# High and low halves of the input in one 512-column product, in two mixer projections and the MLP's first layer

## What is computed

```python
u = rmsnorm(h, mix_norm_w[l])
p = u @ w_in[l]
o_dn = deltanet_group(p[..., :DN_COLS], ...)     # causal conv of 4 taps and silu on q, k, v
o_rw = rwkv7_group(p[..., DN_COLS:], ...)        # p + (token_shift(p) - p) * mu
h = h + concatenate([o_dn, o_rw], -1) @ w_out[l]
h = h + memory_cross_attention(...)
h = h + square(relu(rmsnorm(h, ffn_norm_w[l]) @ ffn_w1[l])) @ ffn_w2[l]
```

## Time and profile before

| what | value |
|---|---|
| runs of the kernel before | 2596.57 us median of 3 (2587.17 to 2599.15) |
| span of the profiled execution | 2589.5 us (the page gives no other time for this execution) |
| TensorE busy | 2270.6 us, 88% |
| VectorE busy | 1329.3 us, 51% |
| ScalarE busy | 796.3 us, 31% |
| mean granted clock of TensorE | 0.919 of 2.4 GHz |
| DeltaNet projection, first to last product | 34.5 to 226.2 us |
| RWKV projection, first to last split product | 313.3 to 454.1 us |
| MLP, first product of the first layer | 972.1 us |

### The profile page before, as it was taken

The page is one execution under the profiler, slowest core; times in us unless marked ns, Lnnn a source line. Parts: engine busy times, 40 slices in busy tenths (PEclk is TensorE's granted clock), DMA queues, the critical chain, the costliest instruction groups (busy, mean ns, idle before and its releaser), DMA issues. The chain is left out here.

```text
span 2589.5 us, 39793 instructions
## 1 busy us (share of the span) xinstructions
PE 2270.6 (88%) x17044; PEld 1833.3 (71%) x17044; DVE 1329.3 (51%) x1574; ACT 796.3 (31%) x933; POOL 21.5 (1%) x62
## 2 busy tenths in 40 slices
PE   7998799788799969999999999969884768888885
PEld 7998799577777649998999989958743424344441
DVE  4776655554452136979788888855532211111112
ACT  4453333311233034334343343454502101111110
POOL 0000000000000000000000000000000000000000
PEclk8999899887799989999999999999997788999997
DMA  5443034100143317988888988843405499999998
GB/s 203 177 195 131 2 138 187 57 2 1 40 189 130 130 76 294 352 320 323 307 327 312 344 320 341 308 164 137 195 1 212 183 429 428 427 422 427 427 427 338
DMA packets 68150, 610.05 MB, mean 236 GB/s; under 512 B 9614, under 2 KB 9870, under 8 KB 16782
## 3 DMA queue, kind: packets, MB, share of 16 engines
q1 hardware_dynamic: 56906, 572.11, 55.3%
q0 software_dynamic: 1872, 23.07, 2.2%
q10 hardware_dynamic: 9216, 12.60, 1.4%
HBM read 674.85 MB, written 14.68 MB: 266 GB/s over the span
## 5 line engine op out<-in xcount | busy, mean ns | idle before, releaser
L2051 ACT ACTIVATE ffn_w_hi<-ffn_raw 128x2048 fp32r<-128x2048 f32 x128 | 245.0, 1915 | 372.1 <-PE psum L2096 368.8
L2058 DVE TENSOR_TENSOR ffn_w_lo<-ffn_raw,ffn_w_hi 128x2048 fp32r<-128x2048 f32 x128 | 292.9, 2292 | 90.7 <-ACT ffn_w_hi L2051 90.7
L2094 PE MATMUL psum<-u_hi,ffn_w_hi 128*128 128x256 f32 x1024 | 293.9, 287 | 15.0 <-DVE ffn_w_lo L2058 13.9
L2805 PE MATMUL psum<-moe_raw,moe_x_t 128*32 128x512 f32 x1536 | 217.3, 697 | 91.2 <-DMA moe_raw<-in_moe 83.7
L2096 PE MATMUL psum<-u_hi,ffn_w_lo 128*128 128x256 f32 x1024 | 293.3, 286 | 0.0
L2095 PE MATMUL psum<-u_lo,ffn_w_hi 128*128 128x256 f32 x1024 | 293.3, 286 | 0.0
L613 DVE SCALAR_TENSOR_TENSOR shared<-mod_raw,c_silu,shared 128x2048 f32<-128x2048 f32 x96 | 225.6, 2350 | 0.0
L2094 PEld LDWEIGHTS psum<-u_hi,ffn_w_hi 128*128 128x128 f32 x1024 | 200.4, 196 | 15.8 <-DVE ffn_w_lo L2058 14.1
L2095 PEld LDWEIGHTS psum<-u_lo,ffn_w_hi 128*128 128x128 f32 x1024 | 200.2, 196 | 0.4
L2096 PEld LDWEIGHTS psum<-u_hi,ffn_w_lo 128*128 128x128 f32 x1024 | 200.2, 196 | 0.0
L2094 PE MATMUL psum<-ffn_w_hi,ffn_hid_hi 128*128 128x512 f32 x512 | 199.4, 390 | 0.0
(11 more groups left out here) (563 smaller groups left out, 4348.2 us busy)
## 6 DMA issues: line engine op xcount, KB each, us to landing
moe_raw<-in_moe SPq DMA_DIRECT2D x96, 2048.0 KB, 17.7
ffn_raw<-in_ffn SPq DMA_DIRECT2D x128, 1024.0 KB, 5.2
ring<-in_stream SPq DMA_DIRECT2D x59, 2048.0 KB, 12.3
mod_raw<-in_mod SPq DMA_DIRECT2D x96, 1024.0 KB, 7.4
moe_raw<-in_moe POOLq DMA_DIRECT2D x48, 2048.0 KB
expert_rows<-moe_stage ACTq DMA_DIRECT2D x192, 64.0 KB, 8.7
x<-in_x SPq DMA_DIRECT2D x2, 1024.0 KB, 5.8
u<-in_mem SPq DMA_DIRECT2D x2, 1024.0 KB, 15.7
```

Of the source, the lines that this page charges most:

```text
L2051: act.activation(self.w_hi[:, number % self.HIGHS], self.raw[:, number % self.RAWS], ACT.Copy)\
L2058: dve.tensor_tensor(self.w_lo[:, number % self.LOWS], self.raw[:, number % self.RAWS], self.w_hi[:, number % self.HIGHS].bitcast(F32), ALU ...
L2094: pe.matmul(out, lhs[0], rhs[0], start=start, stop=False)
L2805: mm = pe.matmul(summed(tile)[strip(q), :], e.x_t[:, tile // 4 % 2, UNIT_KC * u + c, strip(tile % 4)], w[:, c * COLS:(c + 1) * COLS], star ...
```

## The change

In three places the input's high and low parts now lie side by side, chunk by chunk, in one tile of [128, 16, 2, 256]. For the high weights one product of 512 columns over both parts writes a whole bank: columns 0 to 255 hold high x high, columns 256 to 511 high x low. The low weights' product of 256 columns adds to columns 0 to 255. So there are two products per chunk in place of three, and two half banks to be added: ScalarE copies the right half out of PSUM (`rest`), VectorE adds the left half to it (`total`).

```diff
 class SplitTiles:
+        self.u = sb(f"{name}_u", [P, KC, 2, T], F32R)
+        self.u_hi, self.u_lo = self.u[:, :, 0, :], self.u[:, :, 1, :]
+        self.rests = sb(f"{name}_rests", [P, 2, T], F32)
...
-                pe.matmul(out, hi, self.u_hi[:, chunk, :], start=chunk == 0, stop=False)
-                pe.matmul(out, hi, self.u_lo[:, chunk, :], start=False, stop=False)
-                mm = pe.matmul(out, lo, self.u_hi[:, chunk, :], start=False, stop=chunk == KC - 1)
+                pair = self.u[:, chunk].rearrange("p a t -> p (a t)")
+                if chunk == KC - 1:
+                    pe.matmul(both[:, 0:T], lo, self.u_hi[:, chunk, :], start=False, stop=False)
+                    mm = pe.matmul(both, hi, pair, start=False, stop=True)
+                else:
+                    pe.matmul(both, hi, pair, start=chunk == 0, stop=False)
+                    mm = pe.matmul(both[:, 0:T], lo, self.u_hi[:, chunk, :], start=False, stop=False)
...
+    def rest(self, act, x, turn=None):
+        k, at = self.k, self.at
+        act.wait_ge(k.ft_free, at(turn, 8, self.f0 + 3 + x))
+        act.wait_ge(k.ft_done, at(turn, 8, self.f0 + x + 1))
+        act.activation(self.rests[:, x % 2], bank(k, x % 4)[:, T:2 * T], ACT.Copy).then_inc(k.piece_rest, 1)
+
+    def total(self, dve, x, out=None, turn=None):
+        k = self.k
+        dve.wait_ge(k.piece_rest, self.at(turn, 8, self.p0 + x + 1))
+        rest = self.rests[:, x % 2]
+        return dve.tensor_tensor(rest if out is None else out, bank(k, x % 4)[:, 0:T], rest, ALU.add)
...
 deltanet_project, VectorE
             tiles.low(dve, 0, (0, 1))
+            tiles.low(dve, 1, (0,))
             with dve.Fori(0, 3) as i:
-                s.loop(i, 8 * 4)
+                s.loop(i, 8 * 5)
                 for m in range(8):
-                    tiles.low(dve, m + 1, (0,), turn=i)
-                    dve.wait_ge(k.ft_done, i * 8 + f0 + m + 1)
-                    ps = bank(k, m % 4)
+                    tiles.low(dve, m + 1, (1,), turn=i)
+                    s.step(tiles.total(dve, m, turn=i))
+                    s.settle()
+                    ps = tiles.rests[:, m % 2]
...
-                        if lag == 2:
-                            tiles.low(dve, m + 1, (1,), turn=i)
+                        if lag == 3:
+                            tiles.low(dve, m + 2, (0,), turn=i)
...
 deltanet_project, ScalarE
                     tiles.high(act, m + 1, (1,), turn=i)
+                    tiles.rest(act, m, turn=i)
                     tiles.high(act, m + 2, (0,), turn=i)
-                    act.wait_ge(k.dve_sem, i * 32 + d0 + 4 * (m + 1))
+                    act.wait_ge(k.dve_sem, i * 40 + d0 + 5 * (m + 1))
...
 mlp, ScalarE
-                act.activation(f.hid[:], k.psum[:, 0:4, 0:T], ACT.Relu).then_inc(f.taken, 1)
+                act.activation(f.hid[:], k.psum[:, 0:4, T:2 * T], ACT.Copy).then_inc(k.act_sem, 1)
+
+            def squares(e):
                 act.wait_ge(f.taken, e + 1)
+                act.activation(f.hid[:], f.hid[:], ACT.Relu).then_inc(k.act_sem, 1)
+                act.wait_ge(k.act_sem, rectified(e))
                 act.activation(f.hid[:], f.hid[:], ACT.Square).then_inc(f.squared, 1)
...
 mlp, VectorE
+            def total(e):
+                dve.wait_ge(k.act_sem, rest(e))
+                dve.tensor_tensor(f.hid[:], k.psum[:, 0:4, 0:T], f.hid[:], ALU.add).then_inc(f.taken, 1)
```

More of the change, by code:

```diff
@@ L314, in product @@
         pe.wait_ge(k.ft_free, at(turn, 8, self.f0 + x + 1))
-        out = bank(k, x % 4)[:, 0:T]
+        both = bank(k, x % 4)
         for half in range(2):
@@ L862, in _ @@
                     tiles.low(dve, m + 1, (1,))
-                dn.dve_after(dve, m)
+                dn.dve_after(dve, m, tiles)
             s.settle()
@@ L882, in _ @@
                     tiles.high(act, m + 1, (1,))
+                tiles.rest(act, m)
                 dn.act_between(act, m)
@@ L1168, in _ @@
             tiles.input_high(act, u)
-            with act.Fori(0, 3) as i:
+            tiles.high(act, 0, (0, 1))
+            tiles.high(act, 1, (0,))
+            with act.Fori(0, 2) as i:
                 for m in range(8):
-                    tiles.high(act, m, (0, 1), turn=i)
+                    tiles.high(act, m + 1, (1,), turn=i)
+                    tiles.rest(act, m, turn=i)
+                    tiles.high(act, m + 2, (0,), turn=i)
+            for m in range(16, 24):
+                if m < 23:
+                    tiles.high(act, m + 1, (1,))
+                tiles.rest(act, m)
+                if m < 22:
+                    tiles.high(act, m + 2, (0,))
         @block.vector
@@ L1186, in _ @@
             tiles.low(dve, 0, (0, 1))
+            tiles.low(dve, 1, (0,))
             with dve.Fori(0, 2) as i:
-                s.loop(i, 8)
+                s.loop(i, 16)
                 for m in range(8):
-                    tiles.low(dve, m + 1, (0,), turn=i)
-                    dve.wait_ge(k.ft_done, i * 8 + f0 + m + 1)
-                    shift(bank(k, m % 4), k.one_less_mu[:, bass.ds(i * 8 + m, 1)],
+                    tiles.low(dve, m + 1, (1,), turn=i)
+                    s.step(tiles.total(dve, m, turn=i))
+                    s.settle()
+                    shift(tiles.rests[:, m % 2], k.one_less_mu[:, bass.ds(i * 8 + m, 1)],
                           k.cols[:, bass.ds(i * 8 + (COL["mu"][0] + m), 1)],
@@ L1199, in _ @@
                 if m < 23:
[L1200 to L1203, removed]
                     tiles.low(dve, m + 1, (1,))
+                s.step(tiles.total(dve, m))
+                s.settle()
+                shift(tiles.rests[:, m % 2], k.one_less_mu[:, m:m + 1], col(k, "mu", m), mix[:, m, :], mix[:, m, 1:T])
+                if m < 22:
+                    tiles.low(dve, m + 2, (0,))
             for m in range(2):
@@ L2153, in _ @@
                 f.split_high(act, number)
+                if number >= 6:
+                    e, j = order[number - 2]
+                    if (e, j) == (1, 0) or (j == f.HALVES and e < FFN_BLOCKS - 1):
+                        squares(0 if j == 0 else e + 1)
                 mod.copy_after(act, number)
@@ L2171, in _ @@
                     e, j = order[number - 2]
-                    if (e, j) == (1, 0) or (j == f.HALVES and e < FFN_BLOCKS - 1):
-                        hidden(0 if j == 0 else e + 1)
+                    due = 0 if (e, j) == (1, 0) else e + 1 if j == f.HALVES and e < FFN_BLOCKS - 1 else None
+                    if due is not None:
+                        total(due)
                     e, j = order[number - 3]
@@ L2177, in _ @@
                 f.split_low(dve, number)
+                if number >= 6 and due is not None:
+                    hidden(due)
                 mod.sum_after(dve, number)
```

40 lines of the change are left out of this document (25 added, 15 removed).

## The result

The changed kernel takes 2604.53 us (median of 9 runs, 2601.48 to 2616.89), the kernel before 2593.98 (9 runs, 2587.17 to 2600.66) on the same chip: ratio 1.0049 (95% interval 1.003 to 1.0067), which is some 13 us more by the ratio, 10.6 between the medians, inside the range and within 0.5%. The profiled execution of the changed kernel took 2601.8 us, span 2600.1. That the forecast of 2600.7 came so near is partly luck: the median of three runs that it started from was 2.6 us above that of nine, and of the change it had +4.1.

A forecast was written before the change was run, and what follows sets the result against it. The prediction took TensorE to bound the three stages before the change. DeltaNet's loop +23.3, its last tiles -1.7, RWKV -5.1 and MLP -12.4 made +4.1 us on 2596.6, so 2600.7 us, range 2580 to 2618.

The forecast's parts named there:

- the ring: DeltaNet loop: ScalarE and VectorE wait on each other from SiLU to SiLU, 6.53 us per tile against 5.76 before.
- Table loads: DeltaNet loop: ScalarE's table reloads, 1.28 us each, are now paid in the ring, 5 x 1.28 = 6.4 us.
- The first two tiles still run on weights split ahead: DeltaNet loop: only 22 of 24 tiles pay the ring's longer step, 16.9 us.
- the z tiles: Last 8 DeltaNet tiles, behind the loop: no SiLU, a single total, TensorE leads again, -1.7 us.
- A chunk takes 0.2267 + 0.120: TensorE, all three stages: a chunk takes 0.3467 us with the pair against 0.360 before, 0.0133 less.
- the MLP's term: MLP: -13.7 us from cheaper chunks and +1.3 for one exposed wait, together -12.4 us.
- The 2.5 ns of the Trainium skill: Fixed part of a warm matmul by the skill; the three saving terms would be 3.8 us, not 20.5; forecast used 13.3 ns.
- RWKV: RWKV loop: TensorE stays the bound with 0.25 us to spare, -5.1 us, upper bound 0.
- MLP's exposed wait: MLP's second block: its 1.1 us wait for the banks grows by 1.23 and a 0.04 hand-over, +1.3 us.
- Rival 1: DeltaNet loop: TensorE's pauses let the granted clock fall; a third of 24 tiles makes +30 us, 2630 us; chance 0.07.
- Rival 2: All three stages: the pair is no cheaper than two 256-column products, +24.6, 2621 us; chance 0.05.
- Rival 3: DeltaNet loop: ScalarE and VectorE overlap more, ring under 5.76 us, table loads hidden; -19.2, 2577 us; chance 0.08.

The follow-up runs named there:

- experiment 2: Changed kernel with each SiLU in the DeltaNet loop issued one tile later on ScalarE: 2588.1 us, ratio 0.9983 to the kernel before.
- experiment 3: Changed kernel with ScalarE's 24 turns of the DeltaNet loop written out in a row: 2594.83 us, ratio 1.0011 to the kernel before.
- experiments 5 and 6: One-column fold products spread ahead of three tiles: in the kernel before, 2587.19 us; with DeltaNet on three products and the rest paired, 2576.55 us.
- experiment 6: Changed kernel with DeltaNet back on three products and the one-column fold products spread ahead of three tiles: 2576.55 us, ratio 0.9946 to the kernel before.

## Why the prediction was right, and which of its terms were not

- **The bound before, and the ring.** Right: 6.48 to 6.58 us a tile for 6.53, its seams within 0.03 us; opened by moving SiLU (experiment 2).
- **Table loads.** Right in sum: paid in full, 2.85 us a trip's end for 2 x 1.28, and 1.2 at the start (experiment 3), 6.9 in all for 6.4. They don't make two steps of 7.8 us a trip, as forecast, but one of 9.33.
- **"The first two tiles still run on weights split ahead".** Wrong: the ring holds from the first SiLU on. The first two steps are 6.64 and 6.80 us where they were 4.39 and 5.82, +3.2, and the first SiLU itself comes 1.8 us later after the first product (15.29 us, and 13.48 before). Against that the later steps made 21.0 us with the loads, not 23.3. With the z tiles at -2.5 (forecast -1.7) the stage came to +23.6.
- **"A chunk takes 0.2267 + 0.120".** This is the step that failed. Each pace had been read from products of one width in a row, and the change alternates them: 0.3531 in the MLP. There half the saving went, and the MLP's term is -5.6 (experiments 5 and 6), not -12.4; that the profiles showed -10.8 was clock dips like that of the earlier trace rows, which the kernel before had at three folds of its profiled execution and the changed one at one.
- **The 2.5 ns of the Trainium skill** ("TensorE: Matmul & The Clock Gate", section "Wait — 56ns, not 53.3ns?"). The trace goes on disagreeing at the 2.4 GHz level: 13 ns for either width in a row of its own. At the 1.2 GHz level it agrees with what the same section says, that there no fixed part shows (below).
- **RWKV.** -3.8 for -5.1; over the profiles 140.6 and 140.9 with three products, 135.7 to 137.6 with pairs. Here the forecast pace came in about half the tiles: against 5.76 us the tiles 2 to 23 save 3.2, where 0.3531 a chunk throughout would save 2.4 and the forecast 4.7. The 135.7 of experiment 6 has 3 us less at the 1.2 GHz level at its start than the others.
- **MLP's exposed wait.** Right: 2.4 us for 1.1 + 1.27. The forecast didn't have the dip of the clock behind it: 3.4 us at the 1.2 GHz level, which cost some 1.5 us, an estimate from 0.64 and 0.353 us a chunk.
- **Rival 1 (clock falls in the loop).** It did not: 1.00 with TensorE idle for 5.6 of 50 us. The Trainium skill's swings where TensorE pauses between groups ("TensorE: Matmul & The Clock Gate", section "A second HAM failure mode: psum-queue depth-cycling") don't show in this loop either. The clock fell elsewhere: at the folds, behind the MLP's exposed wait, and behind the projection.
- **Rival 2 (no saving).** Half true in the MLP, by another mechanism than the one named. **Rival 3 (ring hidden).** Refuted: 6.48 us a tile, where it needs less than 5.76.

## What to carry to other kernels

Before a helper's output gets one more step, follow the whole way round from an activation to the next one through every engine's instruction order: most of the loss lay in an order of instructions, and moving one of them gave back 18 of 24 us. Take the pace of a mix of instructions from a row of the mix; two paces from rows of one kind each need not add up. And where a stage's gain is read from one profile each, compare the granted clock of the stages first: here the dips that one profile had more of were nearly as large as the gain.

## What the runs showed of the hardware

- At the 1.2 GHz level a pair gains nothing. RWKV's first products in the changed kernel: chunks of 0.64 us (340.64 to 341.28), as long as three 256-column products take at that level.

```profile
340.64 0.63 PE L327 MATMUL psum<-rw_u,rw_w_hi 128*128 128x512 f32 x1
...
341.28 0.63 PE L327 MATMUL psum<-rw_u,rw_w_hi 128*128 128x512 f32 x1
```

- At the 2.4 GHz level wide and narrow products in turn run at one of two paces, 0.347 us a pair, the sum of the bare paces (tiles of 5.55 us in RWKV), or 0.353 (tiles of 5.65 there, and the MLP's plain blocks). In rows of four a chunk of the MLP takes 0.3503, in rows of 16 and 32 0.3473. Why was not settled.
- At a row of one-column products that lasts 3.4 to 4.5 us the granted clock falls in most executions and not in all, by the same code: at 20 of 24 such rows in six profiles, and at 2 of 24 where the row is split in three. The fall comes inside the row or right behind it; the stretch of the earlier trace rows at 1230 to 1232 us lies inside one, which runs from 1228.5 to 1233. Behind the projection the clock falls in seven of thirteen profiles.
